# Sums of squares for the q and k norms: one fp32 pass on TensorE becomes two fp32r passes, with VectorE making the low half

## What is computed

```python
def rms(x):
    xf = x.astype(jnp.float32)
    return (xf * lax.rsqrt(jnp.mean(xf * xf, axis=-1, keepdims=True) + EPS)).astype(x.dtype)

q = rms(qkv[:, :, 0]) * p['na_q_norm']                       # neighbourhood attention, k alike
q = ((rms(cq) * p['mla_cq_norm']) @ p['mla_w_uq'])           # latent attention: compressed q and kv
q_nope = rms(q[..., :MLA_NOPE]) * qg[:MLA_NOPE]              # and again behind the up projection
q = rms(q.reshape(B, T, GQA_KV_HEADS, ..., HEAD_DIM)) * p['gqa_q_norm']
if pos is not None: q = rope_2d(q, *pos)                     # rotary, latent tokens only
```

## Time and profile before

| | us |
|---|---|
| median of 3 runs | 2324.03 |
| the runs | 2322.05, 2324.03, 2324.19 |
| span of the profiled execution | 2322.3 |
| TensorE matmul busy | 2250.2 (97%) |
| VectorE busy | 1338.5 (58%) |
| ScalarE busy | 938.6 (40%) |
| GpSimd busy | 154.4 (7%) |

### The profile page before, as it was taken

How to read it: one execution, slowest core, us unless ns; L and a number is a source line. 1 busy time by engine, 2 the same in 40 slices (tenths; PEclk the granted TensorE clock), 3 DMA queues, 4 the chain that set the end, 5 groups by cost and what they waited for, 6 DMA issues and landing times.

```text
span 2322.3 us, 35196 instructions
## 1 busy us (share of the span) xinstructions
PE 2250.2 (97%) x12956; PEld 1879.7 (81%) x12956; DVE 1338.5 (58%) x1958; ACT 938.6 (40%) x1387; POOL 154.4 (7%) x165
## 2 busy tenths in 40 slices
PE   6999989999999999999999989999999999999999
PEld 4789666888888878888888877777788887888887
DVE  7555576566667465435534566656655566545555
ACT  4454667422223343213312346556643334424332
POOL 0113010000000000000000002210100000000000
PEclk8999999999999999999999999999999999999999
DMA  7121010344444211111211131211055552323323
GB/s 291 55 64 64 28 41 20 110 153 136 142 137 166 73 63 64 64 64 64 64 63 59 60 129 64 70 58 59 11 172 174 170 187 76 99 92 98 97 94 118
DMA packets 58785, 221.26 MB, mean 95 GB/s; under 512 B 6752, under 2 KB 6752, under 8 KB 57904
## 3 DMA queue, kind: packets, MB, share of 16 engines
q1 hardware_dynamic: 44496, 160.46, 21.1%
q0 software_dynamic: 14176, 59.26, 7.7%
HBM read 214.45 MB, written 5.24 MB: 95 GB/s over the span
## 4 chain that ended last, share of the span: by engine, by line
PE 89%; DVE 6%; ACT 2%; issue 2%; DMA 0%; SPq 0%; DVEq 0%; ACTq 0%
PE PS L631 86%; PE PS L959 2%; DVE TM L1568 1%; DVE SM L1837 1%; ACT W_hi L1136 1%; DVE F_lo L1565 1%; DVE W_lo L1565 1%; ACT TM L1136 0%; DVE H_lo L1568 0%; ACT XY L1136 0%; DVE PS L1848 0%; DVE XY L1871 0%; DMA XY<-x_in 0%; DVE XY L1568 0%; ACT H_hi L1136 0%
## 5 line engine op out<-in xcount | busy, mean ns | idle before, releaser
L631 PE MATMUL PS<-H_hi,W_hi 128*128 128x512 f32 (+1 forms) x2256 | 805.6, 357 | 16.2 <-DVE H_lo L1568 5.9
L631 PE MATMUL PS<-H_lo,W_hi 128*128 128x512 f32 (+1 forms) x2256 | 794.0, 352 | 0.0
L631 PE MATMUL PS<-H_hi,W_lo 128*128 128x512 f32 (+1 forms) x2256 | 792.8, 351 | 0.0
L1565 DVE TENSOR_TENSOR W_lo<-W_st,W_hi 128x1024 fp32r<-128x1024 f32 x278 | 342.3, 1232 | 553.9 <-ACT W_hi L1136 552.6
L1136 ACT ACTIVATE W_hi<-W_st 128x1024 fp32r<-128x1024 f32 x278 | 293.6, 1057 | 827.5 <-PE PS L631 827.0
L631 PEld LDWEIGHTS PS<-H_hi,W_hi 128*128 128x128 f32 x2256 | 427.2, 189 | 89.2 <-issue 22.2
L631 PEld LDWEIGHTS PS<-H_lo,W_hi 128*128 128x128 f32 x2256 | 427.4, 189 | 58.5 <-issue 2.6
L631 PEld LDWEIGHTS PS<-H_hi,W_lo 128*128 128x128 f32 x2256 | 427.0, 189 | 57.7
L631 PE MATMUL PS<-F_hi,W_hi 128*128 128x512 f32 (+1 forms) x968 | 343.1, 354 | 9.6 <-DVE XY L1568 3.1
L631 PE MATMUL PS<-F_lo,W_hi 128*128 128x512 f32 (+1 forms) x968 | 340.4, 352 | 0.0
L631 PE MATMUL PS<-F_hi,W_lo 128*128 128x512 f32 (+1 forms) x968 | 339.6, 351 | 0.0
(11 more groups left out here) (131 smaller groups left out, 2009.7 us busy)
## 6 DMA issues: line engine op xcount, KB each, us to landing
W_st<-w_all SPq DMA_DIRECT2D x278, 512.0 KB, 3.5
RA<-w_mod POOLq DMA_DIRECT2D x40, 512.0 KB, 3.7
TM<-w_mod POOLq DMA_DIRECT2D x40, 512.0 KB, 3.7
FA<-w_ada SPq DMA_DIRECT2D x8, 512.0 KB, 15.7
XY<-bias_na POOLq DMA_DIRECT2D x2, 1792.0 KB, 8.1
XY<-x_in SPq DMA_DIRECT2D x4, 768.0 KB, 12.2
x_spill<-XY POOLq DMA_DIRECT2D x1, 3072.0 KB, 10.1
RA<-w_mod SPq DMA_DIRECT2D x5, 512.0 KB, 9.9
```

The source lines that it names most:

```text
L631: return nc.tensor.matmul(o, lhsT, rhs, start=start, stop=stop)
L1565: return nc.vector.tensor_tensor(o, a, b, f)
```

## The change

The sums of squares of all 16 items are made in fp32r. The square is split like the other operands: ScalarE squares into an fp32r buffer (`SQ_HI`, in two tiles of `F_lo` that are free then), VectorE multiplies the tile by itself in fp32 (`SQ`) and subtracts the rounded square (`SQ_LO`, over the same bytes as `SQ`). TensorE multiplies both halves by an fp32r copy `MTR` of the constant matrices, which ScalarE makes with three 128x128 copies in the first norm. 1/192 is not exact in fp32r, so ckv uses the matrix of 1/256 and the factor 4/3 goes into the reciprocal root's scale, the Newton constants and the gains (two more tiny multiplies of `PAR` a layer). In `with_statistics` the sum comes after k-step 5 instead of 3, or after 3 and 7 instead of 2 and 6. On VectorE the new pair for a tile stands ahead of that tile's `W_lo` split, except at the first tile and at nq1 of layer 1.

```diff
@@ statistic (TensorE)
-                pe.wait_ge(S["sq"], base["sq"] + c + len(it.src))
+                if i == 0:
+                    pe.wait_ge(S["mats_r"], 3)
+                pe.wait_ge(S["sq_lo"], base["sq_lo"] + c + len(it.src))
                 wait(pe, "newton", base["newton"] + 2 * i - 1 if i else 0)
-                o0, o1 = it.rows
                 for s0, sn in segs(it.w):
                     for q, (_, r0, r1, mat) in enumerate(it.src):
-                        ins = mm(pair(3)[o0:o1, s0:s0 + sn], MT[r0:r1, mat, o0:o1],
-                                 SQ[(c + q) % 2][r0:r1, s0:s0 + sn], q == 0, q == len(it.src) - 1)
+                        for half in (SQ_HI, SQ_LO):
+                            ins = mm(pair(3)[:, s0:s0 + sn], MTR[r0:r1, mat, :], half[(c + q) % 2][r0:r1, s0:s0 + sn],
+                                     q == 0 and half is SQ_HI, q == len(it.src) - 1 and half is SQ_LO)
@@ with_statistics (TensorE)
-                        stop = (3 if len(due) == 1 else 2) if n == 0 else 7 if x.name == "gk" else 6
+                        stop = (5 if len(due) == 1 else 3) if n == 0 else 7
@@ first_norm (ScalarE)
                 load_root_table()
+                act.wait_ge(S["const_loaded"], 16)
+                for r, m in ((R_ALL, M_256), (R_64, M_64), (R_MLA, M_MLA)):
+                    op(MTR[:, r, :], MT[:, m, :], ACT.Copy).then_inc(S["mats_r"], 1)
                 act.wait_ge(S["sq_pass"], KT)
@@ square (ScalarE)
-                        op(SQ[squares % 2][r0:r1, 0:tiles[t].w], RAW[t % 4][r0:r1, 0:tiles[t].w], ACT.Square
-                           ).then_inc(S["sq"], 1)
+                        raw = RAW[t % 4][r0:r1, 0:tiles[t].w]
+                        op(SQ_HI[squares % 2][r0:r1, 0:tiles[t].w], raw, ACT.Square).then_inc(S["sq"], 1)
@@ in_stage (VectorE)
+                def square_lo(t):
...
+                            dve.wait_ge(S["in_raw"], base["in_raw"] + t + 1)
+                            if squares >= 2:
+                                users = [m for m, it in enumerate(its) for _ in it.src]
+                                dve.wait_ge(S["ss"], base["ss"] + users[squares - 2] + 1)
+                            raw = RAW[t % 4][r0:r1, 0:tiles[t].w]
+                            tt(SQ[squares % 2][r0:r1, 0:tiles[t].w], raw, raw, ALU.mult).then_inc(S["sq_raw"], 1)
+                            dve.wait_ge(S["sq_raw"], base["sq_raw"] + squares + 1)
+                            dve.wait_ge(S["sq"], base["sq"] + squares + 1)
+                            sub(SQ_LO[squares % 2][r0:r1, 0:tiles[t].w], SQ[squares % 2][r0:r1, 0:tiles[t].w],
+                                SQ_HI[squares % 2][r0:r1, 0:tiles[t].w]).then_inc(S["sq_lo"], 1)
+                            squares += 1
...
                     if what == "gemm":
-                        if tiles[t].last:
+                        if t == 0:
+                            used(0, 0, b0 + tiles[t].visit)
+                        square_lo(t)
+                        if t and t != nq1 and tiles[t].last:
                             used(0, 0, b0 + tiles[t].visit)
```

More of the change, by code:

```diff
@@ L56 @@
 M_ONE, M_256, M_192, M_64, M_MLA, M_ID = range(6)
+R_ALL, R_64, R_MLA = range(3)
+FROM_256 = {"ckv": 4.0 / 3.0}
 SH1, SC1, G1, SH2, SC2, G2 = (KT * i for i in range(6))
@@ L262, in in_counts @@
     n_rope = sum(i.rope is not None for i in its)
-    return dict(sq=sum(len(i.src) for i in its), ss=len(its), y0=len(its), y_sq=len(its), newton=2 * len(its),
+    n_sq = sum(len(i.src) for i in its)
+    return dict(sq=n_sq, sq_raw=n_sq, sq_lo=n_sq, ss=len(its), y0=len(its), y_sq=len(its), newton=2 * len(its),
                 in_raw=len(in_tiles(l)), in_zn=sum(i.z for i in its), in_hi=4, in_lo=4, rope_shuf=n_rope,
@@ L333, in hybrid_backbone_kernel @@
         RA = sb("RA", [P, 7680])
+        tm_at = -(-nc.sbuf_base // 32) * 32
         TM = sb("TM", [P, 5, T])
+        TMR = nc.alloc_sbuf_tensor_at("TMR", [P, 2, T], F32R, offset=tm_at)
         PAR, MOD = sb("PAR", [P, N_PAR]), sb("MOD", [P, 2, ADA_T + ADA_1])
@@ L338, in hybrid_backbone_kernel @@
         MT = sb("MT", [P, 6, P])
+        MTR = sb("MTR", [P, 3, P], F32R)
         ROPE = sb("ROPE", [P, 4, SEQ])
@@ L354, in hybrid_backbone_kernel @@
         NU = [SQ[0], SQ[1], NY0]
+        SQ_HI, SQ_LO = [F_lo[:, i, :] for i in range(2)], [TMR[:, i, :] for i in range(2)]
         SH_ROW = [TT[:, P * i:P * i + P] for i in range(2)]
@@ L1581, in used, with newton @@
                     split_lo(b % 2, i * per + (b + 3))
-            def newton(r0, r1, w, n, ss, y, t):
+            def newton(r0, r1, w, n, ss, y, t, part):
                 m, y, t = pair(3)[r0:r1, 0:w], y[r0:r1, 0:w], t[r0:r1, 0:w]
@@ L1589, in newton @@
                 dve.wait_ge(S["ss"], ss)
-                stt(t, m, EPS, t, ALU.add, ALU.mult).then_inc(S["newton"], 1)
+                stt(t, m, EPS * part, t, ALU.add, ALU.mult).then_inc(S["newton"], 1)
                 dve.wait_ge(S["newton"], b + 1)
-                stt(t, t, -3.0, y, ALU.add, ALU.mult).then_inc(S["newton"], 1)
+                stt(t, t, -3.0 * part, y, ALU.add, ALU.mult).then_inc(S["newton"], 1)
                 dve.wait_ge(S["newton"], b + 2)
@@ L1723, in in_stage @@
                 tiles, its, b0, w = in_tiles(l), items(l), done[0], width(l)
-                z = n_lo = n_rope = 0
+                z = n_lo = n_rope = squares = 0
+                def square_lo(t):
+                    nonlocal squares
+                    for tile, r0, r1, _ in (src for it in its for src in it.src):
+                        if tile == t:
+                            dve.wait_ge(S["in_raw"], base["in_raw"] + t + 1)
[9 more added lines that the diff above has]
+                            squares += 1
                 def compressed_lo(i):
@@ L1735, in in_stage @@
                 order, later = events(), None
+                nq1 = next(t for t, x in enumerate(tiles) if x.name == "nq1") if l else None
                 if l:
-                    nq1 = order.index(("gemm", next(t for t, x in enumerate(tiles) if x.name == "nq1")))
-                    order[nq1 - 1], order[nq1] = order[nq1], order[nq1 - 1]
                     uq3 = order.index(("gemm", len(tiles) - 1))
                     order[uq3], order[uq3 + 1] = order[uq3 + 1], order[uq3]
-                for what, t in order:
+                for e, (what, t) in enumerate(order):
+                    if l and order[e + 1:e + 2] == [("gemm", nq1)]:
+                        used(0, 0, b0 + tiles[nq1].visit)
                     if what == "values":
```

30 lines of the change are left out of this document (16 added, 14 removed).

## The result

| | us |
|---|---|
| before, median of 4 | 2323.78 (2322.05 to 2324.19) |
| with the change, median of 4 | 2345.94 (2339.49 to 2354.47) |
| ratio, 95% interval | 1.0106 (1.0091 to 1.012) |
| predicted | 2330.3 (2314 to 2337) |

The account below looks back on a forecast made before the run. The prediction took TensorE, busy almost without a gap in both input stages, as the bound. Start 0.5, layer 0 -2.2 and layer 1 +8.0 gave +6.3 us, so the median 2324.0 became 2330.3 us, range 2314 to 2337.

Parts of the forecast that it names:

- TensorE's gain, 19.4 us: Two fp32r passes replace each fp32 sum on TensorE: 15.3 us saved at 768 wide, 4.1 at 512, 19.4 together.
- Start, +0.5: Three 128x128 copies ahead of the first norm's root delay the first matmuls by 0.5 us (between 0.4 and 0.7).
- The pair's price, 1.95 and 1.32: VectorE's new product and subtraction take 1.95 us per source at 768 wide and 1.32 at 512.
- Layer 1, ckv to nk0, +4.8: In layer 1, VectorE's queue with the new pairs makes TensorE some 4.8 us late at nk0's block.
- nk0 to nq0, 2.2 late at uq0 and 1.4 at nq1: In layer 1 behind nk0, shorter sums give time back: TensorE 2.2 us late at uq0, some 1.4 at nq1.
- nq0's sum 4.3, nq1's 1.6, the token block 3.0: Late in layer 1's stage TensorE waits 4.3, 1.6 and 3.0 us for VectorE there; the stage ends 8.0 us later.
- Layer 0, -2.2: Layer 0's input stage: 8.4 us of new waits against 10.6 saved, so 2.2 us shorter (between -6 and +1).
- The places of the sums: In layer 1, ckv's sum comes two k-steps later (+2.1) but about 1.5 shorter, so its chain is 0.6 us late.
- The signs: Signs of being right included layer 1's token blocks beginning about 6 us later and layer 0's about 2 earlier.
- the fourth rival: In both input stages VectorE's new instructions meet GpSimd, some 16 at 0.9 us; a third reaches TensorE: +5, 2335, chance 0.12.

Follow-up runs that it names:

- experiment 3: The changed kernel without VectorE's pair, both fp32r passes reading the rounded square, and the sums at their old places: 2306.84 us, ratio 0.9926.
- experiment 1: The changed kernel without VectorE's pair, both fp32r passes reading the rounded square, the sums at their new places: 2311.11 us, ratio 0.9951.
- experiments 2 and 10: Changed kernel, sums at old places: 2343.57 us. Changed kernel, shuffle behind next pair, ckv's sum at its old place, split ahead of gk's pair: 2331.53 us.
- experiment 4: The changed kernel with 512-wide matmuls that change nothing filling TensorE's eight longest new waits: 2335.87 us, ratio 1.0068.
- experiment 6: The changed kernel with GpSimd's rotations cut to 8 of 512 tokens: 2321.29 us, ratio 0.9992.
- experiment 8: The changed kernel with VectorE's weight split ahead of the pair at every tile but ckv1 (first and nq1 as they were): 2359.25 us, ratio 1.0155.
- experiment 11: The change in layer 0 alone, with the waiting shuffle behind the next tile's pair; layer 1 as in the kernel before: 2319.9 us, ratio 0.9989.
- experiment 7: The kernel before the change with GpSimd's rotations cut to 8 of 512 tokens: 2320.99 us, ratio 0.9999.

## Why the prediction was right in direction and wrong in size

Term by term; times within a stage are counted from the stage's own start:

- *TensorE's gain, 19.4 us*: right in each instruction (1.50 for two sources of 768 where 1.40 was forecast; 0.47 for one of 512), and 16 of it reach the end once the pair is gone (experiment 3).
- *Start, +0.5*: not to be seen. The three copies took 0.69 together; the first `H_hi` matmul came 0.7 earlier, within the 36.9 to 38.0 that executions here differ by.
- *The pair's price, 1.95 and 1.32*: right where nothing disturbs it (1.85 and 1.33).
- *Layer 1, ckv to nk0, +4.8*: measured 7.2 within the stage. cq1's block was forecast 0.9 late and was 1.1 late (start 1423.28 against 1421.59, less the 0.6 that came with the stage). From there the step failed at kr's, gk's and gq0's shuffles: I gave each pair behind them 1.32 us and the split 1.2, and each such group took some 2.04 more, 6.1 in all, of which 2.4 show at nk0.
- *nk0 to nq0, 2.2 late at uq0 and 1.4 at nq1*: measured about 8.2 and 7.7 (by when ScalarE copies the tiles and values out of PSUM, within the stage). The sums were to give back 2.6 on the way. The lower clock behind nk0's wait took as much: 6 us of work there went at half the clock, 3 us lost by that estimate (1454.67 to 1460.6, the rows above). More than half of layer 1's miss of 11.4 had arisen by uq0.
- *nq0's sum 4.3, nq1's 1.6, the token block 3.0*: measured 5.35, 1.45 and 2.78. The places and the order of sizes were right, but behind nq0's and the token block's the clock was at its lower level. From nq1 to the end of the stage TensorE lost 11.7 where 6.6 were forecast.
- *Layer 0, -2.2*: measured +2.8, and +4.9 without the 2.1 us of clock at the start. nq0's sum waited 3.63 instead of 2.4 and nk0's block 2.81 instead of 1.7, the first behind a lengthened subtraction, the second behind a lengthened subtraction and split, and each has a stretch of lower clock behind it. gq0's sum, forecast at 1.3, waited 1.18.
- *The places of the sums*: I charged 0.6 us for ckv's later sum. Alone it takes 1.8 at cq1's block (2.17 against 0.34, experiments 1 and 3); with the pair there, other waits cover it (experiments 2 and 10).
- *The signs*: the token blocks of layer 1 were to begin some 6 us later and began 17.5 later (1533.06 against 1515.53); those of layer 0 were to begin 2 earlier and began 2.0 later (204.29 against 202.25).

**The steps that failed** are two terms of the sum, both put at nothing: that a new pair and the split behind it meet GpSimd, and that the waits lower TensorE's clock. The queue's waits stood in the forecast, and most of their places were right; both terms made them cost more.

**The first** is the step that priced each pair at 1.95 or 1.32 us and the split behind it at 1.2 wherever they stand, and left their meetings with GpSimd to the fourth rival, "GpSimd and VectorE collide more". Its mechanism is what happened: it foresaw some 16 of the new instructions hit at 0.9 us; eight subtractions and two products of the pairs were, and the eight splits behind them, at 0.97 to 1.07 each. I called it a chance of 0.12, because GpSimd is busy for a fifth to a quarter of the stages, as if the pairs met it at random. They don't: a shuffle is what starts GpSimd, and eight of the pairs stand right behind a shuffle, so these meet it every time. The order of VectorE's queue, which I had beside the text, said so. The Trainium skill (SBUF — State Buffer, Who interferes with whom) says that a VectorE instruction with two SBUF inputs and a GpSimd instruction that reads SBUF block each other; the rows agree. Both sides pay: the three GpSimd instructions behind mq1's shuffle take 1.76, 1.71 and 2.14 us, where undisturbed ones of layer 0 take 1.28.

**The second** is the granted clock, which the prediction named and gave no price, because no row showed it in these stages. The trace of before had it just ahead of the windows of the earlier trace rows, at the start of layer 0's stage (41.00 to 46.40, above). With the change it fell to 1.2 GHz at six idle times of 2.2 to 5.4 us; experiment 4 puts that at 8 to 10 us. That is more than half of the 15.6 us between forecast and measurement: the kernel with the fillers, where the clock holds, took 2335.9, and 5.6 above the forecast are left for the meetings and the rest. That the fourth rival's 2335 lies so near is luck in part: that a third of its 15 us would reach TensorE was a guess, and no run measures that share.

Still open is how the 24.6 us of experiment 6 divide between meetings, shuffles that wait for a rotation, and the lower clock that both bring about: taking the rotations away takes away all of it, and no run fills the waits with the rotations cut.

## What to carry to other kernels

When an instruction is added to a queue, look at what the one ahead of it sets going on another engine: what stood second and third behind a shuffle that starts GpSimd met it every time here, so the mean busy share of the other engine is the wrong measure. When the bound engine is TensorE, a new wait can cost more than its length: the six of 2.2 to 5.4 us behind which the clock fell cost 8 to 10 us more here, some 1.5 each. Filling such waits with matmuls that change nothing took that part back. Look for the lower clock in the whole trace of before, not in a window of it. And a gain on the bound engine is only worth what the chains that run beside it can follow: with the pair gone, 16 of 19.4 us arrived, and with half of the passes gone too, 8.8 of a further 11.4.

## What the runs showed of the hardware that I had not expected

- A VectorE product that begins together with a GpSimd instruction, right behind the shuffle, is not delayed (0.69); the next subtraction takes 1.63 to 1.67 at 512 and 1.90 to 1.94 at 768 instead of 0.69 and 0.96, the split behind it 2.29 to 2.32 instead of 1.22. In experiment 8 the same two places lengthened the product to 1.75 and the subtraction to 1.63: it is the place that decides, not the kind of instruction.
- The granted clock is at its lower level behind an idle time of 2.19 us (nk0, layer 1), yet not behind the 2.35 us ahead of cq's sum in the same stage, where the window from 1436 to 1443 shows 1.00. In other kernels it is at its lower level behind 1.79 us (experiment 11) and 1.45 us (experiment 1). So the length of the last idle time alone does not tell.
- When the granted clock rises at the start of layer 0's stage differs between executions that do the same up to there. In the profiled one of the kernel before it rose at about 46.4 us, in that of the same kernel with its rotations cut (experiment 7) at 40.9, and the ninth matmul spoken of above came 2.0 us earlier there. A difference of 2 us between two profiled spans can be that alone.
